# Third piece of the norm sums moved behind scores and transposes in a differential-attention step

## The reference, cut to what matters

```python
q = apply_partial_rotary(rms_norm_2(q, q_norm_gain[li]), cos, sin)
k = apply_partial_rotary(rms_norm_2(k, k_norm_gain[li]), cos, sin)
...
s = jnp.einsum('bqhcd,bkhcd->bhcqk', qb, k).astype(jnp.float32) * scale
p = jax.nn.softmax(s, axis=-1)
a = p[:, :, 0] - lam_f * p[:, :, 1]
o = jnp.einsum('bhqk,bkhd->bqhd', a, vf)
```

## Time and profile before

| | |
|---|---|
| median of 3 runs | 3491.35 us (3487.02 to 3492.61) |
| profiled execution, its time | 3491.04 us |
| its span, first to last instruction | 3489.2 us |
| mean granted TensorE clock | 0.985 |
| busy: TensorE matmuls | 3322.3 us (95%), 18080 instructions |
| busy: VectorE | 2052.5 us (59%) |
| busy: ScalarE | 1569.8 us (45%) |
| busy: POOL (GpSimd) | 1450.2 us (42%) |
| DMA | 206.31 MB, mean 59 GB/s |

### The profile page before, as it was taken

How to read it: one execution, slowest core, us unless ns; L and a number is a source line. 1 busy time by engine, 2 the same in 40 slices (tenths; PEclk the granted TensorE clock), 3 DMA queues, 4 the chain that set the end, 5 groups by cost and what they waited for, 6 DMA issues and landing times.

```text
span 3489.2 us, 57739 instructions
## 1 busy us (share of the span) xinstructions
PE 3322.3 (95%) x18080; PEld 2717.4 (78%) x18080; DVE 2052.5 (59%) x5228; ACT 1569.8 (45%) x3221; POOL 1450.2 (42%) x1830
## 2 busy tenths in 40 slices
PE   8999999999999999999999999999998999999988
PEld 6888887666788888887666788987886799888866
DVE  5766765666346676765667345166665332676653
ACT  6545443444245545443444244145554332556543
POOL 6555654332624555554332621223344222333352
PEclk9999999999999999999999999999999999999999
DMA  5111112111321111112111222111112422111124
GB/s 154 37 31 36 30 37 59 45 37 31 100 89 57 31 37 30 36 30 64 44 39 31 94 95 79 64 51 27 46 53 66 148 86 68 44 39 45 41 83 149
DMA packets 217930, 206.31 MB, mean 59 GB/s; under 512 B 17948, under 2 KB 185260, under 8 KB 216668
## 3 DMA queue, kind: packets, MB, share of 16 engines
q1 hardware_dynamic: 197536, 137.80, 13.9%
q0 software_dynamic: 12208, 47.03, 3.8%
q10 hardware_dynamic: 7920, 18.19, 1.6%
HBM read 148.04 MB, written 37.01 MB: 53 GB/s over the span
## 4 chain that ended last, share of the span: by engine, by line
PE 72%; DVE 14%; issue 5%; ACT 5%; DMA 2%; POOL 1%; DVEq 0%; SPq 0%; ACTq 0%; POOLq 0%
PE banks L1035 24%; PE banks L1322 7%; PE banks L1256 5%; PE banks L1204 5%; PE banks L1228 4%; PE banks L1409 3%; PE banks L1344 3%; PE banks L1150 2%; PE banks L1400 2%; PE banks L1160 2%; PE banks L1283 2%; PE banks L1172 2%; PE banks L1073 2%; DVE SM L2273 1%; PE banks L1386 1%
## 5 line engine op out<-in xcount | busy, mean ns | idle before, releaser
L1035 PE MATMUL banks<-H,whi 128*128 128x512 f32 x3200 | 1038.0, 406 | 5.0 <-ACT VT L1546 3.9
L1035 PEld LDWEIGHTS banks<-H,whi 128*128 128x128 f32 x3200 | 572.9, 188 | 175.6 <-issue 66.1
L1035 PE MATMUL banks<-H,wlo 128*128 128x512 f32 x1600 | 627.7, 392 | 0.0
L688 POOL CAST whi<-raw 128x1024 fp32r<-128x1024 f32 x150 | 164.3, 1095 | 881.6 <-PE banks L1035 369.4
L691 POOL TENSOR_TENSOR wlo<-raw,whi 128x256 fp32r<-128x256 f32 (+1 forms) x246 | 398.8, 1637 | 12.1
L1322 PE MATMUL banks<-H,whi 128*128 128x346 f32 (+1 forms) x1536 | 377.9, 329 | 2.5 <-ACT VK L1761 1.5
L1035 PEld LDWEIGHTS banks<-H,wlo 128*128 128x128 f32 x1600 | 301.2, 188 | 66.8
L2434 DVE TENSOR_SCALAR_CACHE_REDUCE SP<-banks 128x346 f32<-128x346 f32 (+3 forms) x432 | 200.7, 512 | 222.7 <-PE banks L1387 221.9
L1322 PEld LDWEIGHTS banks<-H,whi 128*128 128x128 f32 x1536 | 269.5, 191 | 9.8 <-issue 6.7
L1688 ACT ACTIVATE SM<-SM,stt 128x256 f32<-128x256 f32 (+1 forms) x256 | 124.8, 488 | 320.0 <-DVE stt L2278 320.0
L2144 DVE TENSOR_TENSOR EX<-EX,QB 128x128 f32<-128x128 f32 (+1 forms) x448 | 249.4, 580 | 1.9
(11 more groups left out here) (311 smaller groups left out, 7384.2 us busy)
## 6 DMA issues: line engine op xcount, KB each, us to landing
raw<-in_w_in SPq DMA_DIRECT2D x148, 512.0 KB, 3.7
raw<-in_w_out SPq DMA_DIRECT2D x64, 256.0 KB, 2.6
XT<-x_resident POOLq DMA_DIRECT2D x18, 512.0 KB, 4.0
x_resident<-XT POOLq DMA_DIRECT2D x18, 512.0 KB, 2.9
raw<-in_w_out SPq DMA_DIRECT2D x18, 512.0 KB, 4.9
RQ<-QR SPq DMA_DIRECT2D x112, 64.0 KB, 2.0
XB<-x_resident POOLq DMA_DIRECT2D x14, 512.0 KB, 4.7
SR<-cat_resident SPq DMA_DIRECT2D x16, 448.0 KB, 3.6
```

What stands on the lines that cost most here:

```text
L688: link(nc.gpsimd.tensor_copy(hi, src))
L1035: last = nc.tensor.matmul(bank(half if bk is None else bk), w[:, slot, k, :], H[:, part, a:a + 512], start=k == 0 and n == 0, stop=k == DT ...
```

## The change

In the steps of heads 1 and 2 the table's "sk" becomes "sk01" in the first text and "sk2" at the head of the second, and "sq" likewise. `items2` now reads the thirds from the name, and a name without digits still means all three. Every item keeps its number, so its bank. Head 0's steps, head 3's and the items ahead of the loop keep their texts.

```diff
 STEPS2 = [[("k0", ""), ("k1", ""), ("k2", ""), ("sk", "q0"), ("q1", "q2"), ("sq", ""), ("w0", ""), ("", ""), ("w1", "")],
-          [("v2 k0", ""), ("", ""), ("vt k1", "k2"), ("sk", "q0"), ("q1", "q2"), ("sq", "g0"), ("g1", ""), ("g2", ""), ("w0", "")],
...
+          [("v2 k0", ""), ("", ""), ("vt k1", "k2"), ("sk01", "sk2 q0"), ("q1", "q2"), ("sq01", "sq2 g0"), ("g1", ""), ("g2", ""), ("w0", "")],
...
     for name in text.split():
-        kind, ch = (name, range(3)) if name in ("sk", "sq", "vt") else (name[0], [int(name[1])])
+        kind = name[:2] if name[:2] in ("sk", "sq", "vt") else name[0]
+        ch = [int(c) for c in name[len(kind):]] or range(3)
         h = other if kind in ("k", "q", "sk", "sq", "w") else own
```

## The result

The changed kernel takes 3520.68 us, the median of 6 runs (3509.33 to 3521.85), against 3491.37 us for the kernel before in the same comparison (6 runs, 3487.02 to 3492.61). The ratio is 1.008, with a 95% interval of 1.0069 to 1.0091: slower by 0.8%, 29 us. The forecast was 3526, the range 3512 to 3537.

The account below looks back on a forecast made before the run. TensorE holds 72% of the chain, but at the sq places it waits through ScalarE and VectorE's `normed2`. The terms 20.3 (sq) + 7.6 (sk) + 6.8 (clock) = 34.7 us gave 3526 us, range 3512 to 3537.

Parts of the forecast that it names:

- Part 1: TensorE's third sum moved behind the transposes: between 0 and 0.81 us, taken as no addition.
- Part 2: ScalarE's third evacuation, Ln and Exp behind the softmax: `normed2` starts 5.07 us later at sq, 4.84 us at sk.
- Part 3: Four sq places: VectorE's queue behind `normed2` passes the full 5.07 us to TensorE's transposes, 20.3 us in all.
- Part 4: Four sk places: ScalarE's third copy makes the values' product 1.9 us later, 7.6 us in all.
- Part 5: Four sq places: TensorE's longer waits lower its clock one step on, 6.8 us in all.
- the 1.70: Time in us lost per sq place to TensorE's lower clock over four microseconds, counted four times.
- the near twin in head 0: Queries' sums at the same step, no item behind: TensorE waited 0.57 and 1.79 us, then the clock halved.
- The bound of nothing: Low bound of the clock term: the clock stayed at 1.00 after waits of 1.58 us and less at 3103.24.
- A: Rival: delays at sq and sk places as forecast, but the clock stays; 3519 us, chance 0.20.
- B: Rival: clock also falls at sk, or twice as long at sq, or POOL's split is awaited; 3533 to 3540, chance 0.15.
- C: Rival: TensorE's queued work absorbs the sq delay; 3499 us, or 3495 to 3498 with the moved sum alone; chance 0.09.
- D: Rival: faster, as softmax and `combine` come earlier at both kinds of place; 3483 us, chance 0.03.

Follow-up runs that it names:

- act_only: Against the kernel before: ScalarE gets the changed order (third evacuation, Ln and Exp behind the softmax), TensorE keeps its old order; 3516.06 us, ratio 1.0097.
- experiment 5: Changed kernel with VectorE's `normed2` for the queries moved from the end of step 5 to the end of step 6; 3529.13 us, ratio 1.0116.
- 6: Kernel before with VectorE's `normed2` for the queries moved to the end of step 6; 3515.96 us, ratio 1.0077.
- sk_only: Against the kernel before: only the keys' sums are split, the queries' stay whole; 3491.55 us, ratio 1.0012.
- sq_only: Against the kernel before: only the queries' sums are split, the keys' stay whole; 3511.21 us, ratio 1.0073.
- pe_only: Against the kernel before: TensorE gets the changed order (third sum behind the transposes), ScalarE keeps its old order; 3504.83 us, ratio 1.0058.
- sk_copy_first: Kernel before with only the keys' sums split, and ScalarE's Ln and Exp on RT behind the third copy; 3502.14 us, ratio 1.0030.
- after_q_late: Changed kernel with `normed2` for the queries at the end of step 6, the same run as experiment 5; 3529.13 us, ratio 1.0116.

## Why the prediction was right

*Part 1, TensorE's moved sum: right.* act_only has the change's delays without it.

*Part 2, `normed2` late by 5.07 and 4.84 us: right.* Against the minimum, which it hangs on now, it is 5.39 - 0.37 = 5.02 us late at the sq place and 5.38 - 0.60 = 4.78 us at the sk place.

*Part 3, 5.07 us at each sq place: right,* 5.00 measured, four times, and down to 0.6 us with `normed2` a step later (experiment 5 against 6).

*Part 4, 1.9 us at each sk place: the mechanism right, the size a little high,* 1.70. The sum had q0's evacuation at 0.43 us and a start at the full end of Exp; it starts 0.98 us behind Exp's start (2439.19 against 2438.21) and the copy 0.34 us later. What the sum had not is that 0.2 to 0.3 us come back one step on: `combine`'s first operation takes 0.91, 0.82, 0.84 and 0.85 us there, against 1.10 us at all four places of the kernel before (2464.31 at the first). POOL's weight split, which the prediction moved and costed at nothing, starts 5.8 us behind the marker of step 4 in place of 3.8, so that its cast and not its subtractions runs beside that operation. sk_only has both (0.84 to 0.90 us), sq_only neither (1.10 us). That goes with the split's start; it was not tried by itself.

*Part 5, the clock: right in kind; that 1.95 us came out near the 1.70 is in part luck.* The fall came behind all four sq places. The two waits were 2.33 and 1.55 us (forecast 2.3 to 3.1, and 2.2: the scores between them took 1.7 us, not 1). The clock fell after the first wait and before the second, and stayed at the lower level for 6.8 us (2474.9 to 2481.7), twice as long as at the near twin in head 0. It cost 1.95 us and not 3.4, because the first 2.2 us of it lay ahead of the transposes, where VectorE's work set the time.

The bound of nothing rested on the earlier trace rows, one of four head starts (heads 1 and 2, both layers) in the kernel before. At the other three the clock fell behind the same waits: at 2423.05 TensorE had waited 1.57 us and at 2424.05 another 0.34, and the window of 2424 has a clock of 0.50. In pe_only it did not fall at any of the four sq places behind 1.41 and 1.79 us, and in sk_copy_first it fell at two of four behind 1.78 us.

The term that failed by size is the assumption that 4 x 1.70 comes on top of everything else: the places' own sum is 33.6 us (34.7 predicted), the medians are 29.3 us apart. In the profiled execution the falls at the three head starts are missing. Counted over those four head starts, the profile of before has 3 falls, that of the changed kernel 0, and those of the ten experiments 0 to 4 each, so much of this varies from one execution to the next; whether the change makes them rarer can't be told from one profile of each kernel, and stays open.

*The rivals.* A: the clock fell, so no. B: no fall at the sk places; at the sq places it did last twice as long, but its first 2.2 us cost nothing. C: the wait on VectorE passed to TensorE whole. D: VectorE did reach `normed2` first, and waits 5.22 us there. The Trainium skill ("TensorE: Matmul & The Clock Gate", section "Loop structure matters more than you think") writes "doesn't break PE warmth" beside a VectorE copy behind which the next matmuls follow immediately. The prediction took that as a rule for waits on VectorE too, which the page doesn't say: here TensorE waited 2.33 us for VectorE, and the clock fell at all four places. In pe_only, with waits of 1.41 and 1.79 us a step apart, it stayed at 1.00.

## What to carry to other kernels

Before moving a piece of a chain behind other work on one engine, look at who waits for the chain's end and what is queued behind that waiter: here 5 us of delay on ScalarE cost 5 us where VectorE's queue had evacuations behind the wait and TensorE had no other work. At the sk place the same delay cost VectorE nothing, because it had 5.5 us of idle time behind; the 1.7 us there came from ScalarE's own queue, where a copy stood behind the moved work. With the waiter a step later the sq places cost 0.6 us. And follow a chain that becomes late to its last consumer: the queries' rotation had 5.1 to 7.8 us to spare, and the later place of `normed2` that freed VectorE used up more than that.

## What the hardware showed beyond that

The granted clock went down while TensorE worked, after one wait and ahead of the next: at about 2474.9 us at the changed kernel's sq place, with work from 2473.85 to 2475.55 and the transposes at 2477.10.

POOL's operations in the rotations do not have one duration. Four of the same form take 2.84 us in the earlier trace rows and 4.86 us in head 0 of after_q_late:

```profile
2388.34 4.86 POOL L897 TENSOR_TENSOR QN<-QN,rope 128x260 f32<-128x260 f32 x4 [20.09 <-DMA SR<-QN]
```

```profile
2388.88 3.01 DVE L2417 TENSOR_TENSOR QN<-QN,KM 64x1040 fp32r<-64x1040 f32 x2
```

Of these four, the first and the last took 0.75 us, and the two in the middle, beside VectorE's `TENSOR_TENSOR QN<-QN,KM`, 1.74 us each. It is not enough that VectorE is at work: over the profiles of all twelve kernels, the 128x260 operations of POOL that lay for the most part beside its evacuations out of a bank (533) took at most 0.77 us, no longer than those beside nothing (819, at most 0.78). Those beside `QN<-QN,KM` (65) had a median of 1.74 us, those beside `combine`'s `SCALAR_TENSOR_TENSOR SP<-SP,st` (103) one of 1.61 us. These are counts over traces; no kernel was run to try it. They bear on the later place of `normed2`, which put the queries' rotation beside such operations.
